# Softmax rows normalised by GpSimd before TensorE's transposes, instead of after the product with v

## The chip, the core and the metric

The kernel runs on one core of a Trainium2 chip. A core has TensorE (PE; PEld is its weight load), VectorE (DVE), ScalarE (ACT), GpSimd (POOL) and SyncE (SP), each of which works through its own instructions in order; semaphores tie them together. SBUF is the working memory, PSUM (eight banks of 128 x 512 float32) holds what TensorE writes. The metric is the device time of one launch in microseconds (us), lower is better; the time before is the median of 3 runs.

## The reference

Two transformer blocks follow one another on 512 tokens of width 1024. The change lies in the first block's two attentions, between their projections and the output projection:

```python
def chunked_relbias_attention(q, k, v, rel_bias):   # out_a, 8 heads of 64
    ...
        sc = jnp.einsum('bihd,bjhd->bhij', q_blk, kb).astype(jnp.float32) * scale
        sc = sc + bias[None]
        sc = jnp.where(valid[None, None, None, :], sc, NEG_INF)
        p = jax.nn.softmax(sc, axis=-1).astype(vb.dtype)
        return jnp.einsum('bhij,bjhd->bihd', p, vb)
...
def block_causal_attention(q, k, v):                # out_b, 8 heads of 96 (64 + 32 rotary), values of 64
    ...
        sc = jnp.where(mask[None, None], sc, NEG_INF)
        p = jax.nn.softmax(sc, axis=-1).astype(v.dtype)
        return jnp.einsum('bhqk,bkhd->bqhd', p, v)
...
        x = x + jnp.concatenate([out_a, out_b], axis=-1) @ w_out[l]
```

## The kernel before

The kernel is written out by hand: each engine has its own program, and semaphores order them. Float32 weights come in slabs of 128 x 1024 through a ring of four; GpSimd splits each slab into a high and a low part (`split`: a TENSOR_SCALAR and a TENSOR_TENSOR), and TensorE makes three passes for each product.

The attention works in 32 **steps** `t = 4p + qb`: `p` is a pair of heads (pairs 0 to 3 of the first attention, 4 to 7 of the second), `qb` a block of 128 queries, `e` (0 or 1) the head of the pair. Step `qb` sees L = 128 (qb + 1) keys, so the steps of a pair have L = 128, 256, 384 and 512. For each step:

- TensorE, `scores(t)`: q times k for both heads, into two banks.
- VectorE, `score_max(t)`: per head adds bias or mask, negates, writes 128 x L to `prob` in SBUF and the row minimum to `row_nmax`.
- ScalarE, `softmax(t)`: per head the exponential in place in `prob`, with the row sum.
- VectorE, `row_recip(t)`: reciprocals of the two heads' row sums, 128 x 2.
- TensorE, `turn(t)`: qb + 1 transposes per head of `prob` into banks 4 and 5; ScalarE copies head 0's bank and VectorE head 1's to `probT` (`keep_turned`).
- TensorE, `values(t)`: v times `probT`, into bank 6, where it gathers the pair's o (the two heads by 64 rows, the four query blocks by 128 columns).

TensorE issues in each turn `i` of its loop: `scores(i+1)`, `turn(i-2)`, `values(i-3)`. So a step's scores stand three turns ahead of its transposes. `turn` waits for the exponentials, and `score_max(t)` for `turn(t-4)`, since `prob` has four places per head.

The exponentials are not normalised in `prob`. The reciprocals are brought to o's layout and multiplied there, once per pair:

- GpSimd, `recips_widened(t)`: spreads the 128 x 2 reciprocals over 2 x 64 columns (`rec_wide`).
- TensorE, `recips_spread(p)`: four transposes of `rec_wide` into bank 7, ahead of `turn(4p+4)`.
- ScalarE, `keep_recips(p)`: bank 7 to `o_scaled` (SBUF).
- VectorE, `out_scaled(p)`: bank 6 times `o_scaled`. The next pair's `values` wait for it.
- ScalarE, `out_hi(p)`, and VectorE, `out_lo(p)`: o's high part `h_hi` and the rest `h_lo`, which the output projection takes.

Beside this GpSimd has rotary work for the second attention, `rope_applied(k)` for k = 0 (32 rows), 1 and 2: three TENSOR_TENSOR of 512 columns each. SyncE then moves the rows to where pairs 4 to 7 want them (`rows_moved`), and `scores(16)` waits for the first of these moves. In the last three turns of the loop TensorE starts the output projection (`out1_begun`, 18 matmuls each, with pairs 0 to 5); then come the parts of pair 6 (9 matmuls) and pair 7 (9 matmuls), which wait for `out_lo(6)` and `out_lo(7)`.

Of the kernel before, what the change touches and what calls it, by code (L numbers as in the profile page):

```python
# [18 lines left out]
P = 128  # L19
# [211 lines left out]
def build(nc, x_in, slabs, ada_in, vec_in, both_in, block1_in, block2_in, rope_in, relb_in, lora_in, g2b_in,  # L231
          y_out):
    ctx = ExitStack()
    with ctx:
# [60 lines left out]
        o_scaled, rec_wide = tmp[:, 2, :], [tmp[:, 3, :], tmp[:, 5, :]]  # L295
# [191 lines left out]

        def score_bank(t, e):

            return bank[4 + 2 * t + e if t < 2 else 2 * (t % 2) + e]  # L490
# [105 lines left out]
        def _(pool):  # L596
# [17 lines left out]
            def recips_widened(t):  # L614

                p, qb, _ = pair_step(t)
                if p >= 2 and qb == 0:
                    pool.wait_ge(S("rows_spread"), p - 1)
# [4 lines left out]
            def rope_applied(k):  # L623

                m, swapped = rotary[k]
                if k == 0:
                    pool.wait_ge(S("rope_in"), 32 + 16 * 10)
                r = slice(0, m.shape[0])
                nc.gpsimd.tensor_tensor(m, m, rope[r, 0, :], ALU.mult).then_inc(S("roped"), 1)
                nc.gpsimd.tensor_tensor(swapped, swapped, rope[r, 1, :], ALU.mult).then_inc(S("roped"), 1)  # L630
                pool.wait_ge(S("roped"), 3 * k + 2)
                nc.gpsimd.tensor_tensor(m, m, swapped, ALU.add).then_inc(S("roped"), 1)
# [43 lines left out]
            for n in range(before * RING, SLAB_AT["out1"] + 3):  # L676
                split(n, n % RING, 16 * (n // RING + 1))
            pool.wait_ge(S("w_split"), SLAB_AT["out1"] + 3)
            pool.wait_ge(S("hd_stat"), len(NORMED))
            for i, (a, b) in enumerate(((32, 64), (64, P))):  # L680
                nc.gpsimd.memset(g2b_t[a:b, :], 0.0).then_inc(S("masks_made"), 1)
                pool.wait_ge(S("masks_made"), 9 + i)
            nc.gpsimd.memset(maskb[:, 0, :], 0.0).then_inc(S("masks_made"), 1)
# [43 lines left out]
        def _(pe):  # L727
# [267 lines left out]
            def recips_spread(p):  # L995


                pe.wait_ge(S("recips"), NT * p + NT)
                if p:
                    pe.wait_ge(S("o_kept"), 2 * p - 1)  # L1000
# [30 lines left out]
            def turn(t):  # L1031

                _, qb, _ = pair_step(t)
                for e in range(2):
                    pe.wait_ge(S("probs"), 2 * t + e + 1)
                    if t >= 1:
                        pe.wait_ge(S(f"probT{e}"), t)
                    for kt in range(qb + 1):
                        last = nc.tensor.transpose(bank[4 + e][:, P * kt:P * kt + P], prob[:, 2 * (t % 4) + e, P * kt:P * kt + P], ident)  # L1039
                    last.then_inc(S(f"turned{e}"), 1)  # L1040

            def values(t):
# [57 lines left out]
            def out1_begun(m):  # L1100

                pe.wait_ge(S("row_nmax"), 2 * (8 * NT - 1 + m // 2))
                if m == 0:
                    pe.wait_ge(S("o_made"), 12)
                product(bank[m], at + m, (at + m) % RING, h_hi, h_lo, ks=range(6), stop=False)

            for i in range(8 * NT + 3):
# [6 lines left out]
                if i >= 6 and i % NT == 2:  # L1114
                    recips_spread((i - 6) // NT)
# [7 lines left out]
            for k in (6, 7):  # L1123
                pe.wait_ge(S("o_made"), 2 * k + 2)
# [1605 lines left out]
```

## Time and profile before

| | us |
|---|---|
| median of 3 runs (lowest, highest) | 1700.57 (1699.32, 1702.35) |
| profiled execution, its own time | 1701.04 |
| its span, first to last instruction | 1699.2 |
| TensorE busy in the span | 1657.6 |
| the attention, first scores to last part of pair 7 | about 483.5 to 585.5 |
| mean granted TensorE clock | 0.991 |

The profiled execution takes 1.84 us more than its span, and 0.47 us more than the median of the runs. A step or a stall is read in the timeline: an instruction's start, its length, and in brackets how long its engine was idle before it and who ended that. Matmul durations overlap (one starts before the one ahead of it has ended), so the time that TensorE gives to a group is read from start to start.

### The profile page before, as it was taken

To read this page: it belongs to the slowest core of one execution; us is meant where nothing else is said; L and a number is where in the kernel's file an instruction comes from. 1 tells how busy PE (TensorE), PEld (TensorE's weight loads), DVE (VectorE), ACT (ScalarE), POOL (GpSimd) and SP (SyncE) were. 2 spreads that over 40 slices of the span, in tenths; PEclk is the share of its full clock that TensorE was granted. 3 is DMA by queue.
4 is the path that set the end of the run, shared out by engine and by line. 5 is a ranking of instruction groups with operands and counts; after the bars stand their busy time and mean duration, and the time that the engine had idled before them with its cause. 6 is when DMAs were issued, how large, how long until landed. Compare 5 with 4: busy or idle time off the path is not lost.

```text
span 1699.2 us, 26804 instructions
## 1 busy us (share of the span) xinstructions
PE 1657.6 (98%) x10118; PEld 1355.5 (80%) x10118; DVE 946.7 (56%) x1389; ACT 433.2 (25%) x721; POOL 981.4 (58%) x596
## 2 busy tenths in 40 slices
PE   8999999999999999999999999998989999999998
PEld 6888888888767778888888867887868788888887
DVE  5666551226656346666562159987766766665103
ACT  4000000015866321111100031234353333233001
POOL 3666666766572377666677744611205576666774
PEclk9999999999999999999999989999999899999999
DMA  6444443333241134444443322210002232233332
GB/s 215 142 147 148 146 144 118 102 100 121 87 120 33 50 106 143 142 147 148 148 150 111 100 87 70 92 64 3 3 2 87 75 96 92 97 99 99 101 110 88
DMA packets 52112, 175.43 MB, mean 103 GB/s; under 512 B 6272, under 2 KB 8704, under 8 KB 51904
## 3 DMA queue, kind: packets, MB, share of 16 engines
q1 hardware_dynamic: 43056, 144.64, 26.3%
q10 hardware_dynamic: 8976, 29.63, 5.5%
q8 instruction: 61, 1.00, 0.3%
q14 instruction: 19, 0.16, 0.0%
HBM read 169.46 MB, written 2.10 MB: 101 GB/s over the span
## 4 chain that ended last, share of the span: by engine, by line
PE 93%; ACT 2%; DVE 2%; issue 1%; POOL 1%; DMA 0%; ACTq 0%; SPq 0%; DVEq 0%; POOLq 0%
PE banks L730 25%; PE banks L732 25%; PE banks L731 25%; PE banks L1199 4%; PE banks L1055 1%; PE banks L1028 1%; PE banks L762 1%; PE banks L1039 1%; PE banks L763 1%; PE banks L768 1%; PE banks L850 1%; PE banks L1025 1%; PE banks L1174 1%; PE banks L803 1%; PE banks L805 0%
## 5 line engine op out<-in xcount | busy, mean ns | idle before, releaser
L602 POOL TENSOR_TENSOR w_lo<-w_raw,w_hi 128x1024 fp32r<-128x1024 f32 x256 | 634.2, 2477 | 21.4
L600 POOL TENSOR_SCALAR w_hi<-w_raw 128x1024 fp32r<-128x1024 f32 x256 | 288.4, 1126 | 555.5 <-DMA w_raw<-in_slabs 477.0
L730 PE MATMUL banks<-h_hi,w_hi 128*128 128x512 f32 x1376 | 540.6, 393 | 0.6 <-POOL w_lo L602 0.6
L732 PE MATMUL banks<-h_hi,w_lo 128*128 128x512 f32 x1376 | 535.7, 389 | 0.0
L731 PE MATMUL banks<-h_lo,w_hi 128*128 128x512 f32 x1376 | 535.6, 389 | 0.0
L730 PEld LDWEIGHTS banks<-h_hi,w_hi 128*128 128x128 f32 x1376 | 258.4, 188 | 60.2 <-issue 5.8
L731 PEld LDWEIGHTS banks<-h_lo,w_hi 128*128 128x128 f32 x1376 | 258.4, 188 | 54.4 <-issue 1.7
L732 PEld LDWEIGHTS banks<-h_hi,w_lo 128*128 128x128 f32 x1376 | 258.3, 188 | 54.1
L730 PE MATMUL banks<-act_hi,w_hi 128*128 128x512 f32 (+1 forms) x550 | 209.7, 381 | 0.0
L731 PE MATMUL banks<-act_lo,w_hi 128*128 128x512 f32 (+1 forms) x550 | 209.3, 381 | 0.0
L732 PE MATMUL banks<-act_hi,w_lo 128*128 128x512 f32 (+1 forms) x550 | 209.3, 381 | 0.0
L730 PEld LDWEIGHTS banks<-act_hi,w_hi 128*128 128x128 f32 x550 | 103.4, 188 | 19.7
L731 PEld LDWEIGHTS banks<-act_lo,w_hi 128*128 128x128 f32 x550 | 103.4, 188 | 19.7
L732 PEld LDWEIGHTS banks<-act_hi,w_lo 128*128 128x128 f32 x550 | 103.4, 188 | 19.7
L2041 DVE TENSOR_TENSOR tmp<-banks,tmp 128x512 f32<-128x512 f32 x44 | 30.5, 692 | 148.2 <-PE banks L732 144.6
L1633 ACT ACTIVATE tmp<-tmp 128x512 f32<-128x512 f32 x44 | 27.9, 634 | 329.5 <-DVE tmp L2041 329.4
L2081 DVE SCALAR_TENSOR_TENSOR xT<-banks,xT 128x512 f32<-128x512 f32 x24 | 16.5, 690 | 165.4 <-PE banks L732 165.4
L2033 DVE TENSOR_TENSOR act_lo<-tmp,act_hi 128x512 f32 x66 | 103.9, 1574 | 8.1
L2055 DVE CUSTOM_DVE_ANT_0 adaw<-adaw,silc 128x1024 f32<-128x1024 f32 x48 | 78.9, 1643 | 5.1 <-DMA adaw<-in_ada 4.8
L2599 DVE SCALAR_TENSOR_TENSOR tmp<-banks,vec,tmp 128x511 f32<-128x511 f32 x44 | 32.8, 746 | 75.9 <-ACT tmp L1933 75.8
L1199 PEld LDWEIGHTS banks<-in_arena 64*64 64x64 f32 x1792 | 59.5, 134 | 10.5 <-issue 6.9
L1199 PE MATMUL banks<-in_arena 64*64 64x64 f32 (+1 forms) x1792 | 62.3, 231 | 5.6 <-issue 2.7
(389 smaller groups left out, 1840.8 us busy)
## 6 DMA issues: line engine op xcount, KB each, us to landing
w_raw<-in_slabs SPq DMA_DIRECT2D x260, 512.0 KB, 3.5
adaw<-in_ada ACTq DMA_DIRECT2D x48, 512.0 KB, 3.6
relb<-in_relb ACTq DMA_DIRECT2D x8, 256.0 KB, 2.9
out_y<-xT SPq DMA_DIRECT2D x16, 128.0 KB, 1.8
w_raw<-in_slabs SPq DMA_DIRECT2D x4, 256.0 KB, 5.2
xT<-in_x SPq DMA_DIRECT2D x1, 1024.0 KB, 8.3
block<-in_block ACTq DMA_DIRECT2D x1, 704.0 KB, 6.1
xT<-in_x SPq DMA_DIRECT2D x2, 256.0 KB, 3.8
```

What stands on the lines that cost most here:

```text
L600: nc.gpsimd.tensor_scalar(w_hi[:, r, :], w_raw[:, r, :], 1.0, 1.0, ALU.mult, ALU.mult).then_inc(S("w_hi"), 1)
L602: nc.gpsimd.tensor_tensor(w_lo[:, r, :], w_raw[:, r, :], w_hi[:, r, :], ALU.subtract).then_inc(S("w_split"), 1)
L730: mm(out, hi, rhs_hi, start=start, stop=False, skip_group_check=True)
L731: mm(out, hi, rhs_lo, start=False, stop=False, skip_group_check=True)
L732: return mm(out, lo, rhs_hi, start=False, stop=stop, skip_group_check=True)
L762: mm(bank[n], w_hi[:, r, w], h_hi[:, k, :], start=k == 0, stop=False, skip_group_check=True)
L1199: last = mm(out, block_of(lhs, operands, e, g, c), r, start=opens and i == 0, stop=i == len(pairs) - 1, skip_group_check=True)
L1633: f(tmp[:, 2 + u, :], tmp[:, 2 + u, :], ACT.Silu).then_inc(S("silu"), 1)
L2033: v.tensor_tensor(actl_t[:, bass.ds(at * T, T)], t, hi, ALU.subtract).then_inc(S("act_lo"), 1)
L2041: v.tensor_tensor(tmp[:, 2 + u, :], bank[2 * u], tmp[:, 0, :], ALU.mult).then_inc(S("gate_scaled"), 1)
L2055: v.tensor_tensor_reduce(out=adaw[:, u, :], in0=adaw[:, u, :], in1=silc, scale=1.0, scalar=0.0, op0=ALU.mult, op1=ALU.add, accum_out=mod_s ...
L2599: v.scalar_tensor_tensor(out=tmp[:, n, 1:T], in0=bank[n][:, 0:T - 1], scalar=w[1], in1=tmp[:, n, 1:T], op0=ALU.mult, op1=ALU.add).then_inc ...
```

## The change

GpSimd multiplies the exponentials by their row's reciprocal, in place, before they are transposed: two TENSOR_SCALAR of 128 x L per step with a scalar from SBUF per row (`probs_scaled`). `turn(t)` now waits for these and not for the exponentials. Widening, spreading, copying and multiplying of the reciprocals are gone. o gathers in bank 6 for even pairs and bank 7 for odd ones; ScalarE and VectorE take the high and low part straight from the bank, and `values` of a pair wait for `out_lo` of two pairs before. `row_recip` comes one place earlier on VectorE, `out_lo(p)` stands where `out_scaled(p)` stood, the last split of a slab ahead of the attention moves behind the first two steps' multiplications, and the nine rotary operations are dealt out one behind each of steps 4 to 6, 8 to 10 and 12 to 14.

```diff
@@ gpsimd
-            def recips_widened(t):
-                ...
-                out = rec_wide[p % 2][:, P * qb:P * qb + P].rearrange("p (e w) -> p e w", e=2)
-                nc.gpsimd.tensor_scalar(out, rec_of(t).unsqueeze(2).to_broadcast([P, 2, CH]), 1.0, None, ALU.mult)                    .then_inc(S("recips"), 1)
+            def probs_scaled(t):
+
                 pool.wait_ge(S("row_recip"), t + 1)
+                for e in range(2):
+                    nc.gpsimd.tensor_scalar(prob_of(t, e), prob_of(t, e), rec_of(t)[:, e:e + 1], None, ALU.mult)\
+                        .then_inc(S("prob_scaled"), 1)
...
-            rope_applied(0)
-            for t in range(8 * NT):
-                if t == NT:
-                    rope_applied(1)
-                    rope_applied(2)
-                    pool.wait_ge(S("roped"), 9)
-                recips_widened(t)
+            for t in range(2, 8 * NT):
+                probs_scaled(t)
+                if NT <= t < 4 * NT and t % NT < 3:
+                    rope_applied(t // NT - 1, t % NT)
@@ tensor
-            def recips_spread(p):
-                ...
-                for qb in range(NT):
-                    b = slice(P * qb, P * qb + P)
-                    last = nc.tensor.transpose(bank[7][:, b], rec_wide[p % 2][:, b], ident)
-                last.then_inc(S("rows_spread"), 1)
...
-                    pe.wait_ge(S("probs"), 2 * t + e + 1)
+                    pe.wait_ge(S("prob_scaled"), 2 * t + e + 1)
...
-                if qb == 0 and p >= 1:
-                    pe.wait_ge(S("o_made"), 2 * p - 1)
+                if qb == 0 and p >= 2:
+                    pe.wait_ge(S("o_made"), p - 1)
...
-                        last = mm(bank[6][CH * e:CH * e + CH, P * qb:P * qb + P], v[:, kt, CH * h:CH * h + CH],
+                        last = mm(bank[6 + p % 2][CH * e:CH * e + CH, P * qb:P * qb + P], v[:, kt, CH * h:CH * h + CH],
@@ scalar
-                f(o_scaled, bank[7], ACT.Copy).then_inc(S("o_kept"), 1)
-
             def out_hi(p):
-                act.wait_ge(S("o_made"), 2 * p + 1)
-                f(h_hi[:, p, :], o_scaled, ACT.Copy).then_inc(S("o_kept"), 1)
+
+                act.wait_ge(S("values"), last_step(p) + 1)
+                f(h_hi[:, p, :], bank[6 + p % 2], ACT.Copy).then_inc(S("o_kept"), 1)
@@ vector
-                v.tensor_tensor(o_scaled, bank[6], o_scaled, ALU.mult).then_inc(S("o_made"), 1)
...
-                v.tensor_tensor(h_lo[:, p, :], o_scaled, h_hi[:, p, :], ALU.subtract).then_inc(S("o_made"), 1)
+
+                dve.wait_ge(S("o_kept"), p + 1)
+                v.tensor_tensor(h_lo[:, p, :], bank[6 + p % 2], h_hi[:, p, :], ALU.subtract).then_inc(S("o_made"), 1)
```

How the change moves VectorE's instructions at the end of pair 0 (from `score_max(7)` of head 1, L = 512, to `keep_turned(5)`, L = 256, and before also `out_lo(0)`). Before:

```order
L2193 ISA prob,small<-banks,relb 128x512 [waits turned1,scores]
L2193 ISA small 128x1
L2208 COPY probT_even<-banks 128x128 [waits values,turned1]
L2214 TENSOR_TENSOR tmp<-banks,tmp 128x512 [waits values,o_kept]
L2200 RECIPROCAL small<-small 128x2 [waits probs]
L2193 ISA prob,small<-banks,relb 128x128 [waits turned0,relb_in0,scores]
L2193 ISA small 128x1
L2193 ISA prob,small<-banks,relb 128x128 [waits turned1,relb_in0,scores]
L2193 ISA small 128x1
L2208 COPY probT_odd<-banks 128x256 [waits values,turned1]
L2218 TENSOR_TENSOR h_lo<-tmp,h_hi 128x512 [waits o_kept]
```

After:

```order
L2177 ISA prob,small<-banks,relb 128x512 [waits turned1,scores]
L2177 ISA small 128x1
L2192 COPY probT_even<-banks 128x128 [waits values,turned1]
L2184 RECIPROCAL small<-small 128x2 [waits probs]
L2197 TENSOR_TENSOR h_lo<-banks,h_hi 128x512 [waits o_kept]
L2177 ISA prob,small<-banks,relb 128x128 [waits turned0,relb_in0,scores]
L2177 ISA small 128x1
L2177 ISA prob,small<-banks,relb 128x128 [waits turned1,relb_in0,scores]
L2177 ISA small 128x1
L2192 COPY probT_odd<-banks 128x256 [waits values,turned1]
```

The subtraction into `h_lo` (`out_lo(0)`) stood behind the maxima of step 8 and the copy of step 5, and stands ahead of both now; the wait that it has (`o_kept`) is for ScalarE's `out_hi(0)`.

ScalarE at the same place (from `softmax(6)`, L = 384, to the copy of step 5). Before:

```order
L1688 ACTIVATE prob,small<-prob,small 128x384 [waits row_nmax,row_recip]
L1688 ACTIVATE prob,small<-prob,small 128x384 [waits row_nmax]
L1707 ACTIVATE tmp<-banks 128x512 [waits roped,rows_spread]
L1698 ACTIVATE probT_even<-banks 128x128 [waits values,turned0]
L1688 ACTIVATE prob,small<-prob,small 128x512 [waits row_nmax,row_recip]
L1688 ACTIVATE prob,small<-prob,small 128x512 [waits row_nmax]
L1724 DMA relb<-in_relb 128x512 x2
L1711 ACTIVATE h_hi<-tmp 128x512 [waits o_made]
L1698 ACTIVATE probT_odd<-banks 128x256 [waits values,turned0]
```

After:

```order
L1681 ACTIVATE prob,small<-prob,small 128x384 [waits row_nmax,row_recip]
L1681 ACTIVATE prob,small<-prob,small 128x384 [waits row_nmax]
L1691 ACTIVATE probT_even<-banks 128x128 [waits values,turned0]
L1681 ACTIVATE prob,small<-prob,small 128x512 [waits row_nmax,row_recip]
L1681 ACTIVATE prob,small<-prob,small 128x512 [waits row_nmax]
L1709 DMA relb<-in_relb 128x512 x2
L1696 ACTIVATE h_hi<-banks 128x512 [waits values]
L1691 ACTIVATE probT_odd<-banks 128x256 [waits values,turned0]
```

The copy from bank 7 to `tmp` (`keep_recips(0)`) is gone; `out_hi(0)` keeps its place behind the exponentials of step 7 and takes bank 6.

GpSimd after the change, from step 2's multiplications (L = 384) on; before, the first three rotary operations stood ahead of all widening and the other six ahead of step 4's:

```order
L625 TENSOR_SCALAR prob<-prob,small 128x384 [waits row_recip]
L625 TENSOR_SCALAR prob<-prob,small 128x384
L625 TENSOR_SCALAR prob<-prob,small 128x512 [waits row_recip]
L625 TENSOR_SCALAR prob<-prob,small 128x512
L625 TENSOR_SCALAR prob<-prob,small 128x128 [waits row_recip]
L625 TENSOR_SCALAR prob<-prob,small 128x128
L635 TENSOR_TENSOR kr<-kr,tmp 32x512 [waits rope_in]
L625 TENSOR_SCALAR prob<-prob,small 128x256 [waits row_recip]
L625 TENSOR_SCALAR prob<-prob,small 128x256
L637 TENSOR_TENSOR tmp<-tmp 32x512
```

Between the multiplications of two steps stands one rotary operation, from step 4 on.

## Rows read from the trace of the kernel before

**Rows 1.** The page's first part: busy us of an engine, share of the span, instructions.
```profile
PE 1657.6 (98%) x10118; PEld 1355.5 (80%) x10118; DVE 946.7 (56%) x1389; ACT 433.2 (25%) x721; POOL 981.4 (58%) x596
```

**Rows 2.** A window in the attention: each engine's busy us (x instructions), granted clock, DMA.
```profile
500.00:520.00 20.00, 20.00 (x184) 13.06 (x182) 14.82 (x57) 14.91 (x49) 12.09 (x16) 1.00 0.32 81
```

**Rows 3.** Timeline, pair 0's end (last row pair 1's): start us, us, engine, line, out<-in, count [idle before].
```profile
500.54 0.66 PE L1003 MATMUL banks<-both,tmp 128*128 128x128 f32 x4
...
500.64 0.69 DVE L2193 CUSTOM_DVE_ANT_0 prob<-banks,relb 128x512 f32<-128x512 f32 x1 [1.10 <-PE banks L1025]
...
501.04 0.38 PE L1039 MATMUL banks<-both,prob 128*128 128x128 f32 x2
...
501.26 0.69 DVE L2193 CUSTOM_DVE_ANT_0 prob<-banks,relb 128x512 f32<-128x512 f32 x1
...
501.89 0.72 ACT L1688 ACTIVATE prob<-prob,small 128x512 f32<-128x512 f32 x1
...
502.56 0.69 DVE L2214 TENSOR_TENSOR tmp<-banks,tmp 128x512 f32<-128x512 f32 x1 [0.40 <-PE banks L1055]
...
502.59 0.72 ACT L1688 ACTIVATE prob<-prob,small 128x512 f32<-128x512 f32 x1
...
503.24 0.27 DVE L2193 CUSTOM_DVE_ANT_0 prob<-banks,relb 128x128 f32<-128x128 f32 x1
...
503.30 0.62 ACT L1711 ACTIVATE h_hi<-tmp 128x512 fp32r<-128x512 f32 x1
...
503.65 0.42 DVE L2208 COPY probT_odd<-banks 128x256 f32<-128x256 f32 x1
...
503.98 0.68 DVE L2218 TENSOR_TENSOR h_lo<-tmp,h_hi 128x512 fp32r<-128x512 f32 x1
...
504.38 0.88 PE L1039 MATMUL banks<-both,prob 128*128 128x128 f32 x6
...
509.51 0.66 PE L1003 MATMUL banks<-both,tmp 128*128 128x128 f32 x4
```

**Rows 4.** Timeline, the same places in pair 5, whose heads have 96 rows.
```profile
550.09 0.60 PE L1003 MATMUL banks<-both,tmp 128*128 128x128 f32 x4
...
550.29 0.69 DVE L2193 CUSTOM_DVE_ANT_0 prob<-banks,maskb 128x512 f32<-128x512 f32 x1 [0.16 <-PE banks L1028]
...
550.53 0.38 PE L1039 MATMUL banks<-both,prob 128*128 128x128 f32 x2
...
554.28 0.82 PE L1039 MATMUL banks<-both,prob 128*128 128x128 f32 x6
```

**Rows 5.** Timeline at the attention's end: TensorE's waits; pair 6's part starts at 581.05.
```profile
563.32 0.20 PEld L1055 LDWEIGHTS banks<-probT_even,vb 128*64 128x64 f32 x4 [0.51 <-DVE tmp L2214]
...
581.05 0.50 PE L730 MATMUL banks<-h_hi,w_hi 128*128 128x512 f32 x1
...
583.37 0.19 PEld L730 LDWEIGHTS banks<-h_hi,w_hi 128*128 128x128 f32 x1 [0.41 <-DVE h_lo L2218]
```

**Rows 6.** GpSimd's groups by shape: count | busy us, mean ns | idle before.
```profile
L621 POOL TENSOR_SCALAR tmp<-small 128x128 f32<-128x128 f32 x32 | 16.6, 526 | 43.6 <-DVE small L2200 43.5
...
L607 POOL TENSOR_SCALAR w_hi<-w_raw 128x512 fp32r<-128x512 f32 x2 | 1.2, 620 | 32.0 <-DMA w_raw<-in_slabs 32.0
...
L629 POOL TENSOR_TENSOR qr<-qr,tmp 128x512 f32<-128x512 f32 x2 | 2.6, 1277 | 0.0
```

**Rows 7.** Timeline at the attention's start, on three engines.
```profile
487.78 1.05 POOL L600 TENSOR_SCALAR w_hi<-w_raw 128x1024 fp32r<-128x1024 f32 x1 [3.38 <-DMA w_raw<-in_slabs]
...
495.71 0.17 DVE L2200 RECIPROCAL small<-small 128x2 f32<-128x2 f32 x1 [0.37 <-ACT prob L1688]
...
497.66 1.09 PE L1039 MATMUL banks<-both,prob 128*128 128x128 f32 x8
```

**Rows 8.** Timeline, SyncE's first DMA of rotary rows for pair 4 and that pair's first scores.
```profile
502.89 0.54 SPq L556 DMA_DIRECT2D qn<-qr  x1
...
520.31 0.49 PE L1028 MATMUL banks<-kn,qn 96*128 96x128 f32 x2
```

More of the change, by code:

```diff
@@ L485, in rec_of, with prob_of, last_step @@
             return row_rec[:, 2 * (t % 8):2 * (t % 8) + 2 * n]
+        def prob_of(t, e):
+            return prob[:, 2 * (t % 4) + e, 0:pair_step(t)[2]]
+        def last_step(p):
+            return NT * p + NT - 1
         def score_bank(t, e):
@@ L675, in _ @@
                     split(i * RING + r, r, i * 16 + 16)
-            for n in range(before * RING, SLAB_AT["out1"] + 3):
+            for n in range(before * RING, SLAB_AT["out1"] + 2):
                 split(n, n % RING, 16 * (n // RING + 1))
-            pool.wait_ge(S("w_split"), SLAB_AT["out1"] + 3)
+            pool.wait_ge(S("w_split"), SLAB_AT["out1"] + 2)
             pool.wait_ge(S("hd_stat"), len(NORMED))
@@ L682, in _ @@
                 pool.wait_ge(S("masks_made"), 9 + i)
+            for t in range(2):
+                probs_scaled(t)
+            split(SLAB_AT["out1"] + 2, (SLAB_AT["out1"] + 2) % RING, 16 * ((SLAB_AT["out1"] + 2) // RING + 1))
             nc.gpsimd.memset(maskb[:, 0, :], 0.0).then_inc(S("masks_made"), 1)
@@ L1038, in turn @@
                     for kt in range(qb + 1):
-                        last = nc.tensor.transpose(bank[4 + e][:, P * kt:P * kt + P], prob[:, 2 * (t % 4) + e, P * kt:P * kt + P], ident)
+                        last = nc.tensor.transpose(bank[4 + e][:, P * kt:P * kt + P], prob_of(t, e)[:, P * kt:P * kt + P], ident)
                     last.then_inc(S(f"turned{e}"), 1)
@@ L1113, in _ @@
                     values(0)
-                if i >= 6 and i % NT == 2:
-                    recips_spread((i - 6) // NT)
                 if 4 <= i < 8 * NT + 2:
@@ L1680, in softmax @@
             def softmax(t):
-                _, _, L = pair_step(t)
                 if t >= 4:
@@ L1686, in softmax @@
                     act.wait_ge(S("row_nmax"), 2 * t + e + 1)
-                    p = prob[:, 2 * (t % 4) + e, 0:L]
+                    p = prob_of(t, e)
                     f(p, p, ACT.Exp, scale=-1.0, bias=of_step(row_nmax, t)[:, e:e + 1],
@@ L1724, in _ @@
                             act.dma_start(relb[:, b, :], relb_in[4 + b]).then_inc(S(f"relb_in{p}"), 16)
-                if i >= 6 and i % NT == 2:
-                    keep_recips((i - 6) // NT)
-                if i >= 7 and i % NT == 3:
-                    out_hi((i - 7) // NT)
+                for p in range(8):
+                    if i == last_step(p) + 4:
+                        out_hi(p)
             norm_squares("ffn2", xT, lambda j: act.wait_ge(S("x_new"), 8 + j + 1))
@@ L2192, in score_max @@
                     added = relb[:, b, T - L:T] if p < 4 else maskb[:, 0, T - L:T]
-                    v.tensor_tensor_reduce(out=prob[:, 2 * (t % 4) + e, 0:L], in0=score_bank(t, e)[:, 0:L],
+                    v.tensor_tensor_reduce(out=prob_of(t, e), in0=score_bank(t, e)[:, 0:L],
                                            in1=added, scale=-1.0, scalar=-LOWEST, op0=ALU.add, op1=ALU.min,
@@ L2208, in keep_turned @@
                 v.tensor_copy(probT[t % 2][:, 1, 0:L], bank[5][:, 0:L]).then_inc(S("probT1"), 1)
-            def out_scaled(p):
-                dve.wait_ge(S("o_kept"), 2 * p + 1)
-                dve.wait_ge(S("values"), NT * p + NT)
-                v.tensor_tensor(o_scaled, bank[6], o_scaled, ALU.mult).then_inc(S("o_made"), 1)
             def out_lo(p):
-                dve.wait_ge(S("o_kept"), 2 * p + 2)
-                v.tensor_tensor(h_lo[:, p, :], o_scaled, h_hi[:, p, :], ALU.subtract).then_inc(S("o_made"), 1)
+                dve.wait_ge(S("o_kept"), p + 1)
+                v.tensor_tensor(h_lo[:, p, :], bank[6 + p % 2], h_hi[:, p, :], ALU.subtract).then_inc(S("o_made"), 1)
             score_max(0)
             score_max(1)
+            row_recip(0)
             for n, t in enumerate((2, 3, 0, 1)):
@@ L2227, in _ @@
                 v.tensor_scalar(va[:, t, :], bank[(t + 2) % 4], n_rs[:, t:t + 1], None, ALU.mult).then_inc(S("in1_raw"), 1)
+                if t == 2:
+                    row_recip(1)
                 if t == 3:
@@ L2232, in _ @@
             keep_turned(1)
-            for i in range(3, 8 * NT + 5):
+            row_recip(2)
+            for i in range(3, 8 * NT + 4):
                 if i < 8 * NT:
@@ L2237, in _ @@
                     keep_turned(i - 3)
-                if i >= 7 and i % NT == 3:
-                    out_scaled((i - 7) // NT)
-                if i >= 8 and i % NT == 0:
-                    out_lo((i - 8) // NT)
-                for t in range(3) if i == 3 else range(i - 1, min(i, 8 * NT)):
-                    row_recip(t)
+                if 4 <= i < 8 * NT + 1:
+                    row_recip(i - 1)
+                for p in range(8):
+                    if i == last_step(p) + 4:
+                        out_lo(p)
             add_half(8, SLAB_AT["out1"], 1, 1.0, "ffn2")
```

35 lines of the change are left out of this document (13 added, 22 removed).

## The prediction

> **What bounds the kernel now.** I read the page's first part, then windows over the attention, then the timeline there. TensorE is busy for 1657.6 us, 98% of the span [rows 1], and in the attention without a gap: 20.00 of 20 us, at granted clock 1.00, where GpSimd has 12.09 and VectorE 14.82 [rows 2]. So an edit is worth what it takes from TensorE's own order, or what it makes TensorE wait; work on the other four engines is free until it is late for TensorE. What follows the attention is TensorE's again, so I carry a gain or loss there to the end one for one.
>
> **What is removed.** The widening of reciprocals on GpSimd (32 instructions, 526 ns each [rows 6]), ScalarE's `keep_recips` and VectorE's `out_scaled` (eight each, 0.69 us for the latter [rows 3]) are hidden today but for the waits below: TensorE's next group starts behind its own last one. What counts is `recips_spread`, eight groups of four transposes. From its start to that of the transposes behind it TensorE gives 0.50 us in the first attention (500.54 to 501.04 [rows 3]) and 0.44 in the second (550.09 to 550.53 [rows 4]): 4 x 0.50 + 4 x 0.44 = 3.76 us.
>
> Two waits of TensorE hang on what is removed. `values(28)` waits for `out_scaled(6)`: its first weight load comes after 0.51 us of waiting, of which I count 0.34, since a third of such a gap stays where the next group has another shape; o's alternate bank takes that wait away. The part of pair 7 waits 0.41 us for `out_lo(7)` [rows 5]. The chain behind the last `values` is out_scaled 0.69, out_hi 0.62, out_lo 0.68 [rows 3]; without the first it is 1.3 us, under the nine matmuls of pair 6, from 581.05 to 583.37 with the wait, so 1.9 at the least [rows 5]. Of the 0.41 I count 0.30, as a change of bank costs something there anyway. Gains: 3.76 + 0.34 + 0.30 = 4.4 us.
>
> **What the new order on VectorE costs.** `out_lo(p)` now stands ahead of `score_max(4p+8)` and the copy of step 4p+5, and waits for `out_hi(p)`, which waits on ScalarE for the two longest exponentials. Queued behind it are the two maxima (L = 128) and that copy, and for the copy waits TensorE: the second half of `turn(4p+6)` wants bank 5. I lay the durations of [rows 3] end to end for pair 0. Maxima of step 7 as before: 500.64, 501.26. Exponentials: the first needs its maximum (501.26 + 0.08 for the accumulator's read + 0.10 for the signal = 501.44) and not ScalarE's copy from bank 7 any more; the two take 0.70 from start to start, so out_hi starts at 502.86 and ends 0.62 later, 503.48. out_lo 503.54, then 0.60 to the next start: 504.14. The maxima of step 8 take 0.41 (503.24 to 503.65): 504.55. The copy, 0.42: 504.97, and with the signal TensorE goes on at 505.07. Before, `turn(6)` started at 504.38 (0.88 us long [rows 3], so its second half some 0.40 later, 504.78); with 0.50 taken out it would reach there at 504.28. So TensorE stands 0.8 us: more than the pair's transposes gave. Pair 1 is the same, 0.8. Behind pair 2 the scores in between are already of heads with 96 rows, which take TensorE longer; I put it half-way between pairs 1 and 3, 0.4. In pairs 3 to 6 nothing: of the same sum in pair 5, the second maximum starts at 550.29 [rows 4], its exponential at 551.08, out_hi 551.8, out_lo 552.5, copy done 553.9, and TensorE wants it at 554.28 + 0.37 - 0.44 = 554.2. Total 2.0 us. The trace of before can't show this wait. Its bounds: nothing, if out_hi comes sooner than I lay it; and 2 x 1.1 + 0.7 + 4 x 0.2 = 3.7, if each of the three signals on the way takes 0.1 more (pairs 3 to 6 have 0.1 to 0.3 to spare).
>
> **What is added on GpSimd.** 64 multiplications of 128 x L, in the path from exponential to transpose. Their price is the term that the trace doesn't show, and these are its bounds. Below: the one-input TENSOR_SCALAR of a slab, 1.05 us for 1024 columns [rows 7] and 0.62 for 512 [rows 6], so 0.19 fixed and 0.84 ns a column: 0.30, 0.41, 0.51 and 0.62 us for the four L. Above: the widening, also a TENSOR_SCALAR, but with one operation and repeated input, 0.526 us for 128 columns [rows 6]; if 0.11 of it is fixed, the rest grows to 0.53, 0.94, 1.36 and 1.77 us. Between lies the rotary TENSOR_TENSOR with two inputs, 1277 ns for 512 [rows 6]. I take the lower price. The multiplication is contiguous as the slab's is, and two blocks of 64 columns at 0.19 + 0.05 each are 0.49, which already nearly explains the widening's 0.526.
>
> In the Trainium skill ("GPSIMD Engine Reference", section 3.1) it stands that loop bodies of up to two operations run at the port's rate, 1.03 cycles per element, and (section 7) that each separate read command costs some 100 cycles that don't overlap. By these the sum would be the lower price's; by the widening's row as it stands it would be the upper one's. The slab's two rows agree with the first (0.84 ns a column), and no run here shows the second by itself.
>
> At the lower price it hides. Per pair GpSimd has 2 x (0.30 + 0.41 + 0.51 + 0.62) = 3.7 us, and 3 x 1.28 = 3.8 of rotary work in pairs 1 to 3: 7.5 against 8.5 that TensorE has for a pair without the spread (500.54 to 509.51 is 8.97 [rows 3], less 0.50). Latency: the tightest is L = 512. At the start, the reciprocal of step 3 is due at 495.71 and done at 495.88; two multiplications from 496.0 end at 497.25, and TensorE wants the first at 497.66, the second at 498.2 [rows 7]. In pair 1 the reciprocal of step 7 (behind the copy, 504.97) is there at 505.2 and TensorE at `turn(7)` some 1.7 us later, the second head 0.5 after that. It is hidden up to about 1.1 us for one of 512 columns; above that each step of 512 holds TensorE.
>
> The last split ahead of the attention (from 487.78, 3.5 us [rows 7]) comes behind four short multiplications that are over by then, and the output projection needs it 85 us later: nothing. The rotary rows of pair 4 come late: k = 1 is done behind step 10, about 513.5, where SyncE issued from 502.89 before. Four DMAs at 0.6 us each are out by 516, and `scores(16)` stands at 520.31 [rows 8]: 4 us to land, nothing. This cover goes first if GpSimd is slow.
>
> **Sum.** 4.4 - 2.0 = 2.4 us gained: 1701.04 - 2.4 = 1698.6 for a profiled execution of that kind, and as the median lies 0.47 lower, **1698.2 us**.
>
> **Rivals.** (1) *GpSimd is the bound*, slower. At the widening's price a pair's multiplications are 9.2 us, with rotary work 13.0, against 8.97 that a pair takes today, and some 10.5 with 96-row heads (an estimate: the place at 550.29 [rows 4] is five pairs behind that at 500.64 [rows 3], two of them at 8.97 and three at a mean of 10.6). Step 3's end at 499.5, 1.4 late: with its spread saved, +0.9. Pairs 1 and 2: +4.0 each. Pair 3: +2.5. In pairs 4 to 6 the second head of the 512 step comes 0.9 late, less 0.44: +1.3. At the end -1.1. Together +11.6, 1712.1 us. It decides from 1.1 us per 512 columns on. For it speaks that the only single-operation TENSOR_SCALAR on this engine is the dear one; against it, that two blocks explain that. (2) *Half-way*: the two-input rate, 1.28 for 512, holds TensorE at each 512 step of the first attention (0.5, 0.9, 0.9, 0.6), which eats the gain: 1701 us, from 1700 to 1704. (3) *VectorE isn't held*, because out_hi is sooner than laid out: the whole 4.4, 1696.2 us. For it: the exponentials' 0.70 is measured with ScalarE's own copy between; against it, out_hi can't pass the exponentials in ScalarE's order.
>
> **Chances.** Forecast 0.46 (its own range 1697 to 1699.5), (3) 0.14, (2) 0.12, (1) 0.28. The measurement can tell about 0.2%, 3.4 us, from no change. Faster by more: (3) and 0.06 of the forecast, 0.20. Slower by more: (1) and 0.03 of (2), 0.31. Within: 0.49. The range must reach into (1), whose share is over 2 in 10, up to its own value: 1695.8 to 1712.
>
> **What would show it.** In the profile after: the GpSimd line with `prob` x64 and its mean by shape (0.30 to 0.62 right, over 1.1 for 512 rival 1); TensorE's waits in the attention named GpSimd (wrong) or VectorE's copy `probT` ahead of the transposes of steps 6, 10 and 14 (right, 0.8, 0.8 and 0.4 us); VectorE idle 1.4 us ahead of `h_lo` for ScalarE; the time from the first scores to the last part of pair 7 at 99.6 us instead of 102; no wait ahead of the part of pair 7; no wait for the moved rows at `scores(16)`. I am wrong if one 512-column multiplication takes over 1.1 us, or if something behind the attention doesn't start earlier with it.

## The result, and the profile after

The changed kernel takes 1707.2 us, the median of 7 runs (1705.92 to 1709.14), against 1700.3 us for the kernel before in the same series (7 runs, 1699.32 to 1702.35): ratio 1.004, 95% interval 1.0029 to 1.0052. It is slower, by 6.9 us. The profiled execution took 1705.92 us, its span is 1704.1. It is the first rival that came, GpSimd as the bound, with a smaller price than the 11.6 us I worked out for it.

The page's first part, against [rows 1]: TensorE works 0.8 us less, GpSimd 52.5 us more.

```profile
PE 1656.8 (97%) x10086; PEld 1350.1 (79%) x10086; DVE 945.2 (55%) x1381; ACT 429.3 (25%) x713; POOL 1033.9 (61%) x628
```

Windows over the attention, the first the same stretch as [rows 2]. TensorE was busy for 20.00 of 20 us there and is for 16.36 now; GpSimd went from 12.09 to 19.57.

```profile
500.00:520.00 20.00, 16.36 (x129) 9.66 (x126) 10.12 (x43) 10.09 (x34) 19.57 (x19) 0.91 0.09 27
...
500.00:510.00 10.00, 7.82 (x69) 4.50 (x66) 5.95 (x25) 4.93 (x17) 10.00 (x10) 1.00 0.18 54
510.00:512.00 2.00, 1.12 (x8) 0.66 (x5) 0.00 (x0) 1.62 (x5) 2.00 (x3) 0.86 0.00 0
512.00:514.00 2.00, 2.00 (x15) 1.56 (x16) 0.76 (x2) 0.16 (x2) 2.00 (x3) 0.50 0.00 0
514.00:516.00 2.00, 2.00 (x13) 0.68 (x12) 0.65 (x3) 0.28 (x1) 2.00 (x3) 0.79 0.00 0
```

GpSimd's groups by shape in the attention. These are the rows that the prediction had no counterpart for: 602, 920, 1240 and 1562 ns for the four lengths, that is 0.28 us fixed and 2.5 ns for each column. The prediction's bounds were 0.30 to 0.62 and 0.53 to 1.77 us.

```profile
L625 POOL TENSOR_SCALAR prob<-prob,small 128x512 f32<-128x512 f32 x16 | 24.8, 1562 | 1.7 <-DVE small L2184 1.7
L625 POOL TENSOR_SCALAR prob<-prob,small 128x384 f32<-128x384 f32 x16 | 19.7, 1240 | 4.9 <-DVE small L2184 4.9
L625 POOL TENSOR_SCALAR prob<-prob,small 128x256 f32<-128x256 f32 x16 | 14.6, 920 | 1.8 <-DVE small L2184 1.8
L625 POOL TENSOR_SCALAR prob<-prob,small 128x128 f32<-128x128 f32 x16 | 9.5, 602 | 0.1
```

The waits in the attention, 483 to 592 us (engine, line, waited for: us in total, times, the longest). TensorE's transposes (L1035) wait for GpSimd. The wait for VectorE's copy that the prediction foresaw three times is seen once, at step 10: GpSimd is later than VectorE at steps 6 and 14.

```profile
PEld banks L1035 <- POOL prob L625: 15.3, 18, 1.4
DVE h_lo L2197 <- ACT h_hi L1696: 15.2, 8, 6.1
...
PE banks L1035 <- POOL prob L625: 7.3, 11, 0.9
...
PE banks L1035 <- DVE probT_odd L2192: 0.6, 1, 0.6
```

The timeline, GpSimd and then TensorE. From 495.89, behind step 3's reciprocal (forecast 496.0), GpSimd goes from one instruction to the next without a gap. The first row holds step 3's two multiplications (L = 512) and step 4's two (L = 128); the second of 512 columns ends at 495.89 + 2 x 1.56 = 499.01, and this is what TensorE waits for at 499.05. Further on step 6 (L = 384) and step 7 (L = 512) are waited for head by head, 0.67 to 0.88 us each.

```profile
495.89 4.26 POOL L625 TENSOR_SCALAR prob<-prob,small 128x512 f32<-128x512 f32 x4 [0.53 <-DVE small L2184]
500.12 1.26 POOL L635 TENSOR_TENSOR kr<-kr,tmp 32x512 f32<-32x512 f32 x1
501.36 1.81 POOL L625 TENSOR_SCALAR prob<-prob,small 128x256 f32<-128x256 f32 x2
503.15 1.26 POOL L637 TENSOR_TENSOR tmp<-tmp 32x512 f32<-32x512 f32 x1
504.40 2.45 POOL L625 TENSOR_SCALAR prob<-prob,small 128x384 f32<-128x384 f32 x2
```

```profile
499.05 0.65 PE L1035 MATMUL banks<-both,prob 128*128 128x128 f32 x4 [0.81 <-POOL prob L625]
...
501.50 0.44 PE L1035 MATMUL banks<-both,prob 128*128 128x128 f32 x2
...
505.69 0.55 PE L1035 MATMUL banks<-both,prob 128*128 128x128 f32 x3 [0.71 <-POOL prob L625]
506.90 0.55 PE L1035 MATMUL banks<-both,prob 128*128 128x128 f32 x3 [0.67 <-POOL prob L625]
...
509.68 0.66 PE L1035 MATMUL banks<-both,prob 128*128 128x128 f32 x4 [0.80 <-POOL prob L625]
511.22 0.96 PE L1035 MATMUL banks<-both,prob 128*128 128x128 f32 x4 [0.88 <-POOL prob L625]
```

**Where the time went.** I read it as a shift: when the same group of matmuls starts in the two profiled executions (501.50 here against 501.04 in [rows 3] is +0.46). "Cost" is the shift behind the attention less that ahead of it.

| place (time before) | shift after | cost of the part | as rival 1 had it |
|---|---|---|---|
| ahead of step 3's transposes (496.81) | -0.08 | | |
| step 3 (501.04) | +0.46 | +0.5 | +0.9 |
| pair 1 (510.00) | +5.25 | +4.8 | +4.0 |
| pair 2 (518.97) | +7.35 | +2.1 | +4.0 |
| pair 3 (529.49) | +9.80 | +2.5 | +2.5 |
| pairs 4 to 6 (561.05) | +9.70 | -0.1 | +1.3 |
| the end (592.12) | +8.65 | -1.1 | -1.1 |

So the attention costs 8.7 us, and the median shows 6.9. The difference has a place of its own, in the second block. From 1190 to 1197 us of the kernel before TensorE's granted clock is 0.50 to 0.55; after, it is 1.00 there, and the shift falls from +7.7 at 1168 to +4.6 at 1229. (Another 0.9 us goes between 970 and 1000, where the clock is at 0.50 for 6.8 us in this execution and for 10.2 in that of the kernel before. There the executions differ whatever the kernel: experiments 6 and 12, whose attention is that of the kernel before to 0.04 us, stand 0.6 earlier and 0.6 later behind it.) Windows of that stretch, the kernel before first, then the changed one:

```profile
1180.00:1200.00 20.00, 17.09 (x454) 15.53 (x455) 12.45 (x29) 4.46 (x9) 9.65 (x6) 0.83 0.02 3
```

```profile
1180.00:1200.00 20.00, 17.94 (x520) 15.10 (x522) 15.02 (x31) 4.66 (x9) 6.76 (x4) 1.00 0.01 3
```

### The profile page after: what moved, and what is told of

It is laid out like the page before. It is cut to its first block, busy times and chain, and to the rows that moved or that the text cites. A ratio compares the mean times of both kernels' runs of the same rounds, so it can differ in the third digit from the quotient of the medians.

```text
span 1704.1 us, 26727 instructions
## 1 busy us (share of the span) xinstructions
PE 1656.8 (97%) x10086; PEld 1350.1 (79%) x10086; DVE 945.2 (55%) x1381; ACT 429.3 (25%) x713; POOL 1033.9 (61%) x628
## 4 chain that ended last, share of the span: by engine, by line
PE 90%; POOL 3%; DVE 2%; ACT 2%; issue 1%; DMA 0%; ACTq 0%; SPq 0%; DVEq 0%; POOLq 0%
PE banks L738 25%; PE banks L740 25%; PE banks L739 25%; PE banks L1193 4%; POOL prob L625 2%; PE banks L770 1%; PE banks L776 1%; PE banks L771 1%; PE banks L858 1%; PE banks L1051 1%; PE banks L1024 1%; PE banks L1168 1%; PE banks L811 1%; PE banks L813 0%; PE banks L812 0%
## 5 line engine op out<-in xcount | busy, mean ns | idle before, releaser
L625 POOL TENSOR_SCALAR prob<-prob,small 128x128 f32<-128x128 f32 (+3 forms) x64 | 68.3, 1081 | 8.5 <-DVE small L2184 8.3
L2030 DVE TENSOR_TENSOR tmp<-tmp 128x512 f32<-128x512 f32 x44 | 65.2, 1482 | 8.6 <-ACT tmp L1627 8.6
```

The lines of the kernel that those rows point to most:

```text
L625: nc.gpsimd.tensor_scalar(prob_of(t, e), prob_of(t, e), rec_of(t)[:, e:e + 1], None, ALU.mult)\
L2030: v.tensor_tensor(tmp[:, 4 + u, :], tmp[:, 2 + u, :], tmp[:, 4 + u, :], ALU.mult)\
```

## The experiments

My theory once the profile was read: the multiplication is dear because it has one operation. Every one-input instruction that I had taken the low price from (the slab's split) has two, `1.0, 1.0, ALU.mult, ALU.mult`; the widening and the new multiplication have one. The rivals: the scalar read from SBUF for each row is dear, or the engine has this rate in the attention whatever the form.

**1 to 3. The form of the multiplication.** Three kernels, each the changed one with line 625 in another form (arguments shortened):

```diff
-  tensor_scalar(prob, prob, rec, None, ALU.mult)
+  tensor_scalar(prob, prob, rec, 1.0, ALU.mult, ALU.mult)       # 1
+  tensor_scalar(prob, prob, 1.0, 1.0, ALU.mult, ALU.mult)       # 2
+  tensor_scalar(prob, prob, 1.0, None, ALU.mult)                # 3
```

> The changed kernel, with GpSimd's multiplication of the exponentials given a second operation (times 1.0, as the slab's split has it); the scalar is still each row's reciprocal from SBUF. Theory A (the single operation is what makes the instruction dear): 512 columns fall from 1562 ns to about 620, TensorE no longer waits for GpSimd, the attention takes about 2 us less than in the kernel before, the whole about 1698. Theory B (the scalar read from SBUF per row is what makes it dear): 512 columns stay at 1.5 us or grow, the whole stays at about 1707. Theory C (any in-place TENSOR_SCALAR costs this beside VectorE): as B.

> As the run with two operations, but both scalars are the constant 1.0, so that nothing is normalised: the form of the slab's split on the data and at the place of the changed kernel. The output's attention part is left unnormalised. Theories A and B both expect about 620 ns for 512 columns and no wait for GpSimd; what remains is the wait of the transposes of steps 6, 10 and 14 for VectorE's copy, 0.8, 0.8 and 0.4 us, and a whole of about 1698 (2.3 us under the kernel before). Theory C expects 1.5 us for 512 columns. If the copy's wait isn't there, the whole comes out at about 1696.

> As the run with two constants, but a single operation with the constant 1.0; the attention is again left unnormalised. Theory A: 512 columns stay at about 1560 ns, the attention as long as in the changed kernel. Theory B: about 620 ns. With the runs before it this separates the count of operations from the origin of the scalar.

GpSimd's groups of 512 and 128 columns in the three, in this order:

```profile
L625 POOL TENSOR_SCALAR prob<-prob,small 128x512 f32<-128x512 f32 x16 | 10.9, 696 | 9.6 <-DVE small L2184 9.6
...
L625 POOL TENSOR_SCALAR prob<-prob,small 128x128 f32<-128x128 f32 x16 | 5.8, 375 | 0.1
```

```profile
L625 POOL TENSOR_SCALAR prob<-prob 128x512 f32<-128x512 f32 x16 | 9.6, 617 | 10.9 <-DVE small L2184 10.9
...
L625 POOL TENSOR_SCALAR prob<-prob 128x128 f32<-128x128 f32 x16 | 4.5, 297 | 0.5
```

```profile
L625 POOL TENSOR_SCALAR prob<-prob 128x512 f32<-128x512 f32 x16 | 23.5, 1486 | 2.7 <-DVE small L2184 2.5
...
L625 POOL TENSOR_SCALAR prob<-prob 128x128 f32<-128x128 f32 x16 | 8.2, 527 | 0.1
```

With two operations a column costs 0.84 ns ((696 - 375) / 384), with one 2.5 ns ((1486 - 527) / 384); the scalar from SBUF adds 75 to 80 ns to an instruction, whatever its length. Times: (1) 1697.84 us (10 runs) against 1701.6 (21), ratio 0.9975, 0.9966 to 0.9985. (2) 1697.39 us, the same ratio and interval. (3) one execution of 1705.12 us. Attention: -2.0, -2.0 and +5.6 us. So one more operation turns the change from a loss into a gain, with the scalar's read as without it. Where GpSimd is late anyway the read costs too: (3), without it, loses 5.6 us where the changed kernel loses 8.7. Figures for the attention come from one profiled execution each; where two kernels should agree they do, to 0.01 us: -2.03 and -2.02 in (1) and (2), -4.11 twice in (5) and (11), 0.03 and 0.04 in (6) and (12).

In (1) the price that I had forecast is nearly real (0.70 us for 512 columns instead of 0.62), so it also shows the wait that I had forecast. Timeline of VectorE and TensorE at the end of pair 0: `out_lo(0)` waits 1.27 us for ScalarE, the copy ends at 503.64, and TensorE is held. By the shift against the kernel before it loses 0.78, 0.77 and 0.41 us at steps 6, 10 and 14, where the prediction had 0.8, 0.8 and 0.4.

```profile
502.20 0.69 DVE L2197 TENSOR_TENSOR h_lo<-banks,h_hi 128x512 fp32r<-128x512 f32 x1 [1.27 <-ACT h_hi L1696]
...
503.22 0.42 DVE L2192 COPY probT_odd<-banks 128x256 f32<-128x256 f32 x1
```

```profile
502.65 0.55 PE L1035 MATMUL banks<-both,prob 128*128 128x128 f32 x3
503.79 0.52 PE L1035 MATMUL banks<-both,prob 128*128 128x128 f32 x3 [0.59 <-DVE probT_odd L2192]
```

**4 and 5. The low part later on VectorE.** `out_lo(p)` stands behind the next pair's first maxima and the copy, about where it stood before; (4) is the changed kernel with this alone, (5) has two operations as well.

```diff
-            for i in range(3, 8 * NT + 4):
+            for i in range(3, 8 * NT + 5):
...
+                if i >= 8 and i % NT == 0:
+                    out_lo((i - 8) // NT)
...
-                for p in range(8):
-                    if i == last_step(p) + 4:
-                        out_lo(p)
```

> The changed kernel, but VectorE takes the low part of o behind the maxima of the next pair's first step and the copy of its second, where it stood before the change. Theory GpSimd (the price of the multiplications decides): gains 1 to 1.5 us, all in pairs 4 to 6, where the exponentials of the 512 step come sooner; TensorE still waits for GpSimd 15 us or so in all; the whole about 1706. Theory VectorE (the order of the low part decides): the loss goes away, 1701 or less.

> Both edits together: two operations in GpSimd's multiplication, and VectorE's low part of o behind the next pair's first maxima and copy. Theory A with the wait for VectorE priced as in the prediction: the 2.0 us of waiting for the copy goes, the whole gain of 4.4 us is left in the attention (shift of what follows it about -4.5 us against the kernel before, -2.0 with two operations alone). Rival: something else is waited for in its place (GpSimd in pairs 1 and 2), and the shift stays at about -3. Whole about 1695 if the kernel before is at 1700.

(4): 1706.48 us (6 runs) against 1701.6, ratio 1.0029, 1.0016 to 1.0042; attention +7.1, that is 1.6 less than the changed kernel's 8.7, of which 1.2 in pairs 4 to 6. (5): **1694.08 us** (5 runs) against 1700.98 (9), ratio 0.9966, 0.9952 to 0.9979; attention -4.1, so the order on VectorE is worth 2.1 us where GpSimd isn't late. Its window is TensorE's alone again, though GpSimd works 18.12 of the 20 us:

```profile
500.00:520.00 20.00, 20.00 (x184) 13.10 (x183) 15.20 (x62) 15.72 (x50) 18.12 (x26) 1.00 0.20 55
```

**6. The widening with two operations.** The kernel before, one argument changed: `..., 1.0, 1.0, ALU.mult, ALU.mult` in `recips_widened`. It tests the sentence on which I had chosen the low price, that two blocks of 64 columns explain the widening's 526 ns.

> The kernel before, with a second operation (times 1.0) in the widening of the reciprocals. Theory A (a single operation costs some 2.5 ns a column, two 0.83): the widening of 128 columns falls from 526 ns to about 300, and nothing else changes. My reading before (two blocks of 64 columns with a fixed cost each): it stays at about 500 ns.

```profile
L621 POOL TENSOR_SCALAR tmp<-small 128x128 f32<-128x128 f32 x32 | 9.2, 296 | 50.5 <-DVE small L2200 50.4
```

296 ns, with the same two blocks and the same repeated input. The sentence was wrong; the 526 ns of [rows 6] were the single operation. One execution took 1700.2 us, and the attention's shift is 0.0.

**7 to 10. What in the changed kernel the price hits.** Either GpSimd's total work for a pair, 2 x (0.60 + 0.92 + 1.24 + 1.56) + 3 x 1.26 = 12.4 us in pairs 1 to 3, or the length of one step. One execution each. In 7 to 9 some lengths L keep the single operation; in 10 all do, and the nine rotary operations are cut to 16 columns.

```diff
+  *((None, ALU.mult) if t % NT == 3 else (1.0, ALU.mult, ALU.mult))     # 7: 512 dear
+  *((None, ALU.mult) if t % NT < 2 else (1.0, ALU.mult, ALU.mult))      # 8: 128, 256 dear
+  *((1.0, ALU.mult, ALU.mult) if t % NT == 3 else (None, ALU.mult))     # 9: 128 to 384 dear
+  tensor_tensor(m[:, 0:16], m[:, 0:16], rope[r, 0, 0:16], ALU.mult)     # 10, and the other two alike
```

> Two operations everywhere but for the steps of 512 columns, which keep the single one (1.56 us). If the latency of the longest step decides, most of the wait for GpSimd stays: TensorE waits for it at each 512 step, the shift behind the attention is about +2 to +3 us. If only the sum of GpSimd's work per pair decides (6.9 us with 3.8 of rotary work is 10.7, over 8.5), pairs 1 and 2 alone lose, about 2 us each, and pairs 4 to 6 nothing.

> The mirror image: the single operation at 128 and 256 columns (0.60 and 0.92 us), two at 384 and 512. By the latency of the longest steps nothing is lost: the shift behind the attention stays at -2.0 us as with two operations everywhere. If any growth of GpSimd's sum is paid for, it is nearer to 0.

> The changed kernel with the second operation given to the 512-column multiplications alone; the other three lengths keep the dear single-operation form (602, 920 and 1240 ns). Nothing is left out. GpSimd then has 2 x (0.60 + 0.92 + 1.24 + 0.69) + 3 x 1.26 = 10.7 us of work for each of pairs 1 to 3, as much as with 384 and 512 dear together and more than the 9.5 us with 512 dear alone, but no long step ahead of a pair's last transposes. Theory A (what the price costs in the first attention is the engine's total work, more than about 9 us for a pair): TensorE is late by more than with 512 dear alone (+2.2 us from first scores to output projection), about +4. Theory B (it is the latency of the longest step, the total comes into it only where a long step follows): my hand schedule gives +0.2 us against the kernel before, that is 2.2 above the version with all multiplications cheap (-2.0), and GpSimd waits of TensorE only at steps 6, 10 and 14 (L = 384).

> The changed kernel with all multiplications dear, and the nine rotary operations on 16 of 512 columns, so most of the rotary embedding of the second attention's queries and keys is left out. GpSimd has 8.6 us of multiplications for a pair and next to nothing beside them, under the 9 us that TensorE takes. Theory A (the engine's total work is what costs in pairs 1 to 3, with the rotary operations in it): the loss of 8.7 us falls to that of the latencies alone, +2.4 us by my hand schedule, about what 512 dear alone gave (+2.2). Theory B (the dear multiplications hold TensorE by themselves, whatever stands between them): the loss stays above 6 us.

| dear lengths | rotary | GpSimd for a pair, us | attention | against all cheap |
|---|---|---|---|---|
| none (1) | full | 8.1 | -2.0 | 0 |
| 128, 256 (8) | full | 9.4 | -2.0 | 0 |
| 512 (7) | full | 9.8 | +2.2 | +4.2 |
| 128 to 384 (9) | full | 10.7 | +0.5 | +2.5 |
| all (10) | 16 columns | 9.3 | +2.2 | +4.2 |
| all (the change) | full | 12.4 | +8.7 | +10.7 |

The waits of TensorE for GpSimd in (7) and in (10):

```profile
PE banks L1035 <- POOL prob L625: 2.3, 4, 0.8
```

```profile
PE banks L1035 <- POOL prob L625: 2.1, 3, 0.8
```

Against what was expected: (7), (8) and (9) came out near the theory of the longest step (+2 to +3, -2.0, +0.2), and (9) far from the +4 of the theory of total work; (10) came out by the total (+2.4), and not above 6. So both theories have their part, and the table parts them. The length of a pair's last step costs 4.2 us ((7) and (10) alike, though one has the rotary work and the other has the short lengths dear). Total work, with the 512 step cheap, costs 2.5 us at 10.7 us a pair (9), and nothing at 9.4 (8). In (9) GpSimd has no gap from 495.4 to 529.2 us:

```profile
495.40:529.20 33.80, 30.49 (x255) 19.03 (x255) 20.93 (x86) 22.41 (x74) 33.80 (x37) 1.00 0.21 57
```

TensorE waits for it there at steps of L = 384, and it isn't their own length that does it: in (10) they are as dear, and its three waits for GpSimd stand at L = 512. TensorE itself takes some 9.2 us for such a pair in these versions (8.97 of [rows 3], less the spread's 0.44, with some 0.7 of waiting for VectorE's copy). My hand schedule had +0.2 for (9), so it had this part 0.3 too small. Of the change's 8.7 us, 6.5 go with the nine rotary operations (10): they lift the work of pairs 1 to 3 from 9.3 to 12.4 us.

**11 and 12. The stretch in the second block.** Each of the ten versions with the change is 1.8 to 3.1 us shorter from 1168 to 1229 us than the kernel before; (6), whose TensorE program is the old one, is 0.2 us shorter. Only in the kernel before and in (6) does TensorE stand idle inside it, from about 1187 on, for 1.3 and 1.0 us, and for nothing that the profile names. At the same line the changed kernels wait for VectorE instead, 0.5 to 1.0 us. The kernel before:

```profile
1188.30 0.31 PE L1420 MATMUL banks<-in_h 64*64 64x64 f32 x4 [1.28 <-issue]
```

The gain goes with the granted clock. It is at 0.50 for 6.8 us in this stretch in the three versions that don't gain (the kernel before, (6) and (12)), for 3.4 us in the seven that gain 1.8 to 2.5 us, and nowhere in the four that gain 2.9 to 3.1 (the changed kernel, (5), (7) and (11)). In (1), one of the seven:

```profile
1187.50:1190.90 3.40, 3.22 (x52) 2.85 (x54) 3.01 (x8) 0.28 (x1) 0.42 (x1) 0.50 0.02 5
```

I took the idle time for the supply of TensorE's instructions: the change takes some out, so what follows stands elsewhere in the stream. The test puts empty ones at the head of TensorE's program, 64 in (5) for (11), 192 in the kernel before for (12).

```diff
             mm = nc.tensor.matmul
+            for _ in range(64):         # 192 in (12)
+                pe.nop(nofuse=True)
```

> The version with two operations and the late low part, and 64 empty instructions at the head of TensorE's program, where TensorE waits 7 us for its first data anyway. Nothing is left out. It is about a stretch far behind the attention: in both profiled executions of programs with the kernel before's TensorE code TensorE stands 1.0 to 1.3 us in the second block ahead of the matmuls of line 1420 and waits for nothing that the profile shows ('issue'), and its granted clock is then 0.50 for some 6 us; in all ten of programs with the change that idle time is absent and this stretch is 1.8 to 3.1 us shorter. Theory A (the place in the instruction stream decides: the change took 32 transposes, so 64 records, out of TensorE's program, and what supplies its instructions comes late at other places now): with 64 empty instructions ahead the idle time comes back at the same matmuls, the stretch loses 2 to 3 us again, and the median is about 1696.5 instead of 1694.1. Theory B (it hangs on something else in the change, as the times at which the engines come there): no idle time there, 1694 us.

> The kernel before with 192 empty instructions at the head of TensorE's program. Nothing is left out. The trace shows instruction transfers of some 16 KB each (nine packets, 0.15 MB, between 1150 and 1200 us), which would be 256 instructions of 64 bytes; 192 more are then in the same place of such a block as 64 fewer. Theory A (place in the instruction stream): the idle time of 1.3 us ahead of line 1420's matmuls is gone, the stretch from 1184 to 1200 us is 2 to 3 us shorter, and the median is about 1698.5 against 1701 for the kernel before. Theory B: the idle time is there as before, 1701 us. If the empty instructions take longer than the 7 us that TensorE waits at its start, the first matmul comes later, and this is taken off.

(11): 1694.1 us (9 runs) against 1701.01 (18), ratio 0.9965, 0.9955 to 0.9975; 0.2 us of such idle time at that line, and the stretch 2.9 us shorter. (12): 1701.38 us (10 runs), ratio 1.0001, 0.9992 to 1.0011; the idle time is there, 1.3 us ahead of the same matmuls:

```profile
PE banks L1422 <- issue: 1.3, 1, 1.3
```

That looks like the end of the theory of the place in the stream, but the traces show that neither run tested it. The instruction transfers (queue q8, 16 KB each, one for every 125 matmuls or so) begin behind the same matmuls with the empty instructions as without: behind 4899, 5023 and 5149 in the kernel before and in (12), behind 4907, 5031 and 5170 in (5) and in (11). At the 256 instructions that a transfer was taken to hold, 192 more ahead should have moved them by some 96 matmuls, and 64 by 32. They did move with the change: all eleven versions with it agree to 6 matmuls, and so do the three without. Whether the empty instructions reached TensorE at all the traces don't show: the count of instructions is the same with them as without, 26804 in the kernel before and (12), 26727 in (5) and (11). So the theory is open, neither shown nor refuted. That the gain comes with the change is what eleven profiled executions show against three. (11) is also a second series of the best version, with the same time.

## Why the prediction was wrong

**The step that failed** is the price of the multiplication: "I take the lower price. The multiplication is contiguous as the slab's is, and two blocks of 64 columns at 0.19 + 0.05 each are 0.49, which already nearly explains the widening's 0.526." Experiment 6 refutes the explanation (296 ns with the same blocks), and 1 to 3 show what stands in its place: the number of operations. I had the fact in hand. Rival 1 says that "the only single-operation TENSOR_SCALAR on this engine is the dear one", and I weighed it below an arithmetic that happened to come out at 0.49. The upper bound from the widening was within 14% for each length (1.77 against 1.56 us for 512, and for 128, where it was 0.53, below the 0.60 measured). By the prediction's own sign, over 1.1 us for one of 512 columns, it was wrong. Why one operation takes longer than two isn't shown.

With the slope per column from the trace, what I took from the Trainium skill can be put in its place. The Trainium skill ("GPSIMD Engine Reference", section 3.1) has bodies of up to two operations at 1.03 cycles per element. For two operations the runs agree (0.84 ns a column, an estimated 1.0 cycle at the 1.2 GHz that the Trainium skill states in section 1 under the same title). For one they don't: 2.5 ns, three times that. The measurement decides.

**The gains on TensorE's order** were right. With the price repaired and VectorE's order as before, (5) gives 4.1 us in the attention where I had 4.4. The part between is in the spreads of pairs 1 to 3, which gave 0.38 to 0.44 us each in (11) instead of 0.50. The wait of `values(28)` gave 0.35 (0.34 forecast), pair 7's part 0.29 (0.30). That a third of the first wait stays (0.51 waited, 0.35 gained) was in no row when it was forecast.

**VectorE's order** was right in place and size: 2.0 us forecast, 2.1 measured between (1) and (5), and each of the three places as forecast (0.78, 0.77 and 0.41 us). ScalarE kept `out_lo` waiting for 1.27 us where I had 1.4, and TensorE's second half of `turn(6)` came 1.14 us behind the first, so some 0.7 late (half of that group takes 0.44) where I had 0.8. Rival 3 is thereby out. In the changed kernel the same order costs only 1.6 us (between (4) and it), since GpSimd is late there anyway.

**That the price hides up to about 1.1 us per 512 columns**: the price of the two operations, 0.70, hides; at 1.56 it doesn't. The point itself was not tried.

**Rival 1's size.** 8.7 us in the attention against 11.6. By the table the difference is 0.4 in step 3, 1.2 in pairs 1 to 3 (9.3 instead of 10.5; the multiplications of a pair are 8.65 us and not 9.2) and 1.4 in pairs 4 to 6, where a 512 step holds TensorE for 0.4, which the missing spread gives back, instead of 0.9. I had spread the loss evenly over pairs 1 and 2; pair 1 took 4.8 and pair 2 only 2.1. That goes with a stretch of half clock in pair 1: the matmuls from 507.12 to 508.98 us of the kernel before, 1.87 us, took 3.39 in the changed one (511.22 to 514.61). In (4) such a stretch falls into pair 2 (519.0 to 522.4), and the two pairs cost 3.2 us each. What it adds to the 8.7 in all isn't known.

**What was hidden** stayed hidden: the later split, the rotary rows' DMAs (no wait at `scores(16)`), the copies taken off ScalarE.

**That what follows is carried one for one** was wrong by about 2 us. The shift of +8.65 becomes +7.6 behind 1000 us and +4.6 behind 1229, and in the medians the changed kernels stand 1.8 to 2.8 us lower than their attention says (-6.9 against -4.1 for (5), +6.9 against +8.7 for the change).

## What to carry to other kernels

Ask of a price not only for the same engine and type, but for the same form down to the number of operations; where two rows of one opcode differ by a factor that geometry is made to explain, change one argument and see before choosing. When an engine beside the bound takes work into the path, compute both its total for a round against the bound's time and the length of its longest step. An instruction moved ahead in an engine's order carries its wait along to everything behind it. And when a test is to move something, look in its trace whether that moved, before its outcome is read: the empty instructions of (11) and (12) left the instruction transfers where they were.

## What the runs showed of the hardware that I had not expected

- On GpSimd a TENSOR_SCALAR with one operation (a multiplication, on 128 partitions; no other was tried) takes 2.5 ns for each column of float32, one with two operations 0.84 ns, so a second multiplication by 1.0 makes 512 columns 2.2 times as fast (1562 to 696 ns). A scalar of its own for each row adds 75 to 80 ns to an instruction. With one operation and a constant, 512 columns (1486 ns) take longer than a TENSOR_TENSOR of 512 with its two inputs (1277 ns [rows 6]).
- Inside the attention the granted clock of the changed kernel lay at 0.50 (1.2 GHz) from 511.4 to 514.8 us. Ahead of this TensorE had been busy for 1.64 of 3 us (505 to 508) and 1.20 of 2 (508 to 510), with no single wait over 0.9 us; in (10), where it was busy for 3.77 of 5 us (504 to 509), the clock stays at 1.00. I had not counted a wait's price in clock. Its share in the 8.7 us was not measured apart.
- A 1.3 us stop of TensorE with no named cause, in the second block of the kernel before, went away with a change 600 us ahead of it, and of the 6.8 us of half clock behind it 3.4 or nothing was left. The cause is open: the empty instructions that were to test one did not move the instruction transfers.
